# Attention probabilities scaled ahead of their transposes, instead of the attention output after its accumulation

## The chip, the cores and the metric

The kernel runs on one core of a Trainium2 chip. The metric is the device time of one execution in microseconds (us), as a median of several runs. A core has five engines with a queue each: TensorE (PE, matmuls and transposes), VectorE (DVE), ScalarE (ACT), GpSimd (POOL) and SyncE (SP, which issues most DMAs). Each engine takes its instructions in the order of the program; engines wait for one another on semaphores. TensorE reads SBUF and writes PSUM, which has eight banks of 128 x 512 fp32 here, all of them named in this kernel.

## The reference

Two layers over 512 tokens of width 1024. Each layer normalizes x, projects it (`w_in`), runs a recurrent group (RG-LRU) on half of the width and sparse attention (NSA) on the other half, gates both with silu, multiplies by `w_out` and adds x. A final norm follows. The attention part, cut to what the change touches:

```
o_cmp = softmax(q kc^T) vc          # 31 compressed positions
o_slc = softmax(q_rot ks^T) vs      # selected blocks: all of them at this length
o_win = softmax(q_rot kw^T) vw      # window of 512: plain causal at this length
gates = sigmoid(gate_logits)        # 3 per head and token
y_nsa = gates[0]*o_cmp + gates[1]*o_slc + gates[2]*o_win
y     = y_nsa * silu(g_nsa)         # then y @ w_out
```

There are 8 query heads of 64 in 2 key groups of 4. The gate and one over the row sum of the exponentials are one number per token, head and branch.

## The kernel before, in words

Everything follows one list of steps, `schedule()`. Each engine walks through the whole list and runs its own share of each step, so a step's place in the list is its place in every engine's queue. Projections are split in high and low fp32r parts, three matmuls for a product (L1351 to L1353), with weight chunks loaded by SP, split by ACT (`HI`, L774) and DVE (`LO`, L983).

`attention(l)` (L69) lists the attention of a layer. There are 16 units (tile `i` of 128 queries, branch `b` 0 or 1, pair of heads); a unit has four heads and `W = 128*(i+1)` keys. Unit by unit:

- `S` (two steps, r = 0 and 1): PE makes scores of two heads in the two `s_ps` banks (L1410, L1413), DVE takes their minimum (L1259), ACT the exponential into `probs` with its row sum (L928, which shows as an ACTIVATE and a read of the accumulator). `S` of unit u+1 is woven into the steps of unit u, at 0.2 and 0.6 of its length.
- `T`: for each 128 keys PE transposes the four heads' `probs` into a `t_ps` bank (L1426). The first `T` of a unit waits for all four exponentials of it. ACT and DVE in turn copy the bank into one of three `probsT` buffers (L937, L1267).
- `W`: PE multiplies `probsT` by the values (L1462) into an output bank. `C` steps are the same for the compressed branch (L1431), whose probabilities `CS2` has scaled already.
- `K`: DVE makes gate over row sum for the 8 heads of a tile and branch (L1271, L1274) and spreads it over 64 columns a head (L1276). `T` with `B`: PE transposes that spread tile (L1436), ACT copies it to `upad` (L947).
- `O`: DVE multiplies the output bank of a branch with it and sums the branches in `E` (L1285 to L1291). So a query tile has three accumulation groups, alternating between `o_ps` and `a_ps`.
- `Y`, `YH`, `YL`: once the last `O` of a tile is done, DVE multiplies by silu (L1297), ACT and DVE split the result in high and low (L866, L1165).

Between these, `fill()` puts pieces of other matmuls of the layer (`F`, and `G` of the last layer, L1372 to L1374), so that PE has work while the attention's chain runs: per unit four, later three and two pieces in layer 0, five and later four in layer 1. Eight pieces follow the last unit. `put_later` places the steps that come some positions behind another one. After layer 0, PE's `ON` pieces need all `YL` of the layer; after layer 1, the last tile's `G` pieces do (L1364).

Of the kernel before, what the change touches and what calls it, by code (L numbers as in the profile page):

```python
# [28 lines left out]
P = 128  # L29
# [20 lines left out]
N_STAGE, N_RING, N_PT, N_E, N_SWP = 4, 3, 3, 6, 2  # L50
# [18 lines left out]
def attention(l):  # L69
# [27 lines left out]
    def put_later(steps):  # L97
# [9 lines left out]
        def finish(n, i):  # L107
            due.setdefault(n, []).append(("Y", l, i))
            due.setdefault(n + 2, []).append(("YH", l, "n", i))
            due.setdefault(n + 5, []).append(("YL", l, "n", i))  # L110

        n = 0
        while n < len(steps) or any(at >= n for at in due):
            if n < len(steps):
# [27 lines left out]
            if n >= len(steps) and waiting and not any(at >= n for at in due):  # L142
# [4 lines left out]
                   [("CS2", l)], *fill(per_unit[-1] - 2)])  # L147
    for u, (i, b, pair) in enumerate(units):
        main = []
        for k in range(i + 2):  # L150
            if k <= i:
                main.append([("T", l, ("P", i, b, pair, k))])
            if k == 0 and pair == 1:
                main[-1].append(("K", l, i, b))
# [113 lines left out]
class Plan:  # L268


    def __init__(self, sched):
# [5 lines left out]
        for st in sched:  # L277
# [24 lines left out]
            elif k == "O" and st[3] == 0:  # L302
# [34 lines left out]
        self.data = [key for key in self.turns if key[1] != "B"]  # L337
        self.data_no = {key: n for n, key in enumerate(self.data)}
        self.groups = [st[1:] for st in sched if st[0] == "O"]
        self.group_no = {key: n for n, key in enumerate(self.groups)}  # L340
        self.coefs = [st[1:] for st in sched if st[0] == "K"]
        self.coef_no = {key: n for n, key in enumerate(self.coefs)}

# [33 lines left out]
def hybrid_trunk(nc, x, norm_g, w_in, conv_w, conv_b, lru_wa, lru_ba, lru_wi, lru_bi, lru_lambda,  # L377
# [5 lines left out]
    rope_no, unit_no, turn_no, data_no, group_no = plan.rope_no, plan.unit_no, plan.turn_no, plan.data_no, plan.group_no  # L383

    ctx = ExitStack()
    with ctx:
# [15 lines left out]
        probsT = sb("probsT", [P, N_PT + 1, SEQ])  # L402
# [21 lines left out]
        mn, rs, coef = sb("mn", [P, 2, 4]), sb("rs", [P, 2, 8]), sb("coef", [P, 8])  # L424
# [14 lines left out]
        sq_tmp, sq_acc, spread_c = swp[:, 0, :], upad[:, CONV_W - 1:], upad[:, CONV_W - 1:]  # L439
# [4 lines left out]
        wide_c = probsT[:, N_PT, :]  # L444
# [36 lines left out]
        min_ok, exp_ok, coef_ok, spread_ok, o_done = sem("min_ok"), sem("exp_ok"), sem("coef_ok"), sem("spread_ok"), sem("o_done")  # L481
# [58 lines left out]
        def wait_turned(eng, key):  # L540

            d = data_no[key]
            eng.wait_ge(pt_dve if d % 2 else pt_act, d // 2 + 1)

        def wait_turn_bank(eng, n):

            if n >= 2:
                old = plan.turns[n - 2]
                if old[1] == "B":
                    eng.wait_ge(spread_ok, plan.coef_no[(old[0], old[2], old[3])] + 1)  # L550
                else:
                    wait_turned(eng, old)

        def o_bank(l, i, b):

            return o_banks[group_no[(l, i, b)] % 2]
# [143 lines left out]
        def _(pool):  # L700
# [51 lines left out]
            for st in sched:  # L752
# [4 lines left out]
                elif kind == "NORM":  # L757
                    root(st[1])
                elif kind == "FMEAN":
# [5 lines left out]
        def _(act):  # L765
# [45 lines left out]
            for st in sched:  # L811
# [85 lines left out]
                elif kind == "TURNE":  # L897
                    _, l, name = st
                    act.wait_ge(a_full, aux_no[("TURN", l, name)] + 1)
                    if l >= 1:  # L900
                        act.wait_ge(pv_done, per_layer(plan.data, l))
# [9 lines left out]
                elif kind == "S":  # L911
# [3 lines left out]
                    if r == 0:  # L915
# [6 lines left out]
                        if pair == 0 and (i >= 1 or l >= 1):  # L922
                            act.wait_ge(coef_ok, plan.coef_no[(l, i - 1, b) if i >= 1 else (l - 1, TT - 1, b)] + 1)
                    for g in range(N_KV):
                        n, j = 4 * u + 2 * r + g, 2 * g + r
                        act.wait_ge(min_ok, n + 1)
                        col = 2 * (2 * pair + r) + g
                        act.activation(probs[:, 4 * (u % 2) + j, 0:W], s_ps[g][:, 0:W], ACT.Exp, scale=-1.0,  # L928
                                       bias=mn[:, u % 2, j:j + 1], accum_out=rs[:, b, col:col + 1]).then_inc(exp_ok, 1)
                elif kind == "T":  # L930
                    key = (st[1], *st[2])
                    if key[1] != "B" and data_no[key] % 2 == 0:
                        n, d, rows = turn_no[key], data_no[key], P if key[1] == "P" else NC
                        act.wait_ge(t_full, n + 1)
                        if d >= N_PT:
                            act.wait_ge(pv_done, d - N_PT + 1)
                        act.activation(probsT[0:rows, d % N_PT, :], t_ps[n % 2][0:rows, :], ACT.Copy).then_inc(pt_act, 1)  # L937
                    elif key[1] == "B":
                        l, _, i, b = key
                        act.wait_ge(t_full, turn_no[key] + 1)  # L940
                        if b == 1:
                            act.wait_ge(o_done, group_no[(l, i, 0)] + 1)
                        elif i == 0:
                            act.wait_ge(conv_ok, CT * (l + 1))
                        else:
                            act.wait_ge(o_done, group_no[(l, i - 1, 1)] + 1)
                        act.activation(spread_c, t_ps[turn_no[key] % 2][:, :], ACT.Copy).then_inc(spread_ok, 1)  # L947
# [15 lines left out]
        def _(dve):  # L963
# [135 lines left out]
            for st in sched:  # L1099
# [160 lines left out]
                elif kind == "T":  # L1260
                    key = (st[1], *st[2])
                    if key[1] != "B" and data_no[key] % 2 == 1:
                        n, d, rows = turn_no[key], data_no[key], P if key[1] == "P" else NC
                        dve.wait_ge(t_full, n + 1)
                        if d >= N_PT:
                            dve.wait_ge(pv_done, d - N_PT + 1)
                        dve.tensor_copy(probsT[0:rows, d % N_PT, :], t_ps[n % 2][0:rows, :]).then_inc(pt_dve, 1)  # L1267
                elif kind == "K":
                    _, l, i, b = st
                    dve.wait_ge(exp_ok, 4 * (unit_no[(l, i, b, 1)] + 1))  # L1270
                    link(dve.reciprocal(coef[:, :], rs[:, b, :]))  # L1271
                    gate = gates[:, i, :].rearrange("p (g r b) -> p b r g", g=N_KV, b=3)[:, 1 + b, :, :]
                    c8 = coef[:, :].rearrange("p (r g) -> p r g", g=N_KV)
                    link(dve.tensor_tensor(c8, c8, gate, ALU.mult))  # L1274
                    c = coef[:, :].rearrange("p (h a) -> p h a", a=1).to_broadcast([P, 2 * GROUP, HD])
                    dve.tensor_copy(wide_c.rearrange("p (h a) -> p h a", a=HD), c).then_inc(coef_ok, 1)  # L1276
                elif kind == "O":
                    _, l, i, b = st
                    y = e_slot((l, f"y{i}"))
                    if b < 2:  # L1280
                        dve.wait_ge(spread_ok, plan.coef_no[(l, i, b)] + 1)
                    dve.wait_ge(pv_done, data_no[(l, "P", i, b, 1, i) if b < 2 else (l, "C", i, 1)] + 1)
                    if b == 0:
                        wait_e((l, f"y{i}"))
                        dve.tensor_tensor(y, o_bank(l, i, b)[:, :], spread_c, ALU.mult).then_inc(o_done, 1)  # L1285
                    elif b == 2:
                        dve.wait_ge(o_done, group_no[(l, i, 0)] + 1)
                        dve.tensor_tensor(y, y, o_bank(l, i, b)[:, :], ALU.add).then_inc(o_done, 1)
                    else:
                        link(dve.tensor_tensor(spread_c, o_bank(l, i, b)[:, :], spread_c, ALU.mult))  # L1290
                        dve.tensor_tensor(y, y, spread_c, ALU.add).then_inc(o_done, 1)  # L1291
                elif kind == "Y":
# [3 lines left out]
                    dve.wait_ge(o_done, group_no[(l, i, 1)] + 1)  # L1296
                    dve.scalar_tensor_tensor(out=e, in0=e, scalar=0.5, in1=silu_g[:, :, i * P:(i + 1) * P],  # L1297
                                             op0=ALU.mult, op1=ALU.mult).then_inc(ynsa_ok, 1)
# [29 lines left out]
        def _(pe):  # L1328
            def z_piece(key, p):
# [85 lines left out]
            def turn(key):  # L1415
# [4 lines left out]
                if key[1] == "P":  # L1420
                    _, _, i, b, pair, k = key
                    u = unit_no[(l, i, b, pair)]
                    if k == 0:
                        pe.wait_ge(exp_ok, 4 * (u + 1))
                    for j in range(4):
                        ins = pe.transpose(bank[:, j * P:(j + 1) * P], probs[:, 4 * (u % 2) + j, k * P:(k + 1) * P], ident[:, :])  # L1426
                elif key[1] == "C":
# [4 lines left out]
                else:  # L1432
                    _, _, i, b = key
                    pe.wait_ge(coef_ok, plan.coef_no[(l, i, b)] + 1)
# [182 lines left out]
```

## Time and profile before

| | us |
|---|---|
| median of 3 runs | 629.15 (627.08 to 630.05) |
| the profiled execution, its own time | 629.98 |
| its span, first to last instruction | 628.3 |
| PE busy | 584.3 |
| DVE busy | 402.6 |
| ACT busy | 294.1 |
| POOL busy | 16.0 |

Attention steps fill about 148 to 300 us (layer 0) and 447 to 612 us (layer 1) of the span. "Busy" counts overlapping matmuls once. An instruction's mean is its duration, not its distance from the next of its kind: pipelined ones overlap. "idle [x <-releaser]" is the time in which the engine had nothing to run before an instruction, and what ended it.

### The profile page before, as it was taken

To read this page: it belongs to the slowest core of one execution; us is meant where nothing else is said; L and a number is where in the kernel's file an instruction comes from. 1 tells how busy PE (TensorE), PEld (TensorE's weight loads), DVE (VectorE), ACT (ScalarE), POOL (GpSimd) and SP (SyncE) were. 2 spreads that over 40 slices of the span, in tenths; PEclk is the share of its full clock that TensorE was granted. 3 is DMA by queue.
4 is the path that set the end of the run, shared out by engine and by line. 5 is a ranking of instruction groups with operands and counts; after the bars stand their busy time and mean duration, and the time that the engine had idled before them with its cause. 6 is when DMAs were issued, how large, how long until landed. Compare 5 with 4: busy or idle time off the path is not lost.

```text
span 628.3 us, 8688 instructions
## 1 busy us (share of the span) xinstructions
PE 584.3 (93%) x3207; PEld 409.1 (65%) x3207; DVE 402.6 (64%) x690; ACT 294.1 (47%) x586; POOL 16.0 (3%) x32
## 2 busy tenths in 40 slices
PE   4999999889999989998999999999899999999994
PEld 3776777667556555555788677777776666555563
DVE  4786966776555664755576679667664766557532
ACT  3647654424444452543453574462344545445522
POOL 1000000000000000000230000000000000000000
PEclk9999999998999998999899999998999999999999
DMA  8755393343111110101232745734421112000112
GB/s 243 201 155 152 87 231 85 84 102 104 56 34 34 34 35 1 34 0 35 67 101 70 198 122 145 142 82 99 110 74 35 34 39 64 0 2 1 34 34 68
DMA packets 94889, 50.71 MB, mean 81 GB/s; under 512 B 42992, under 2 KB 92288, under 8 KB 94848
## 3 DMA queue, kind: packets, MB, share of 16 engines
q1 hardware_dynamic: 91456, 45.95, 28.9%
q10 hardware_dynamic: 3392, 4.21, 2.5%
q8 instruction: 26, 0.43, 0.3%
q14 instruction: 15, 0.12, 0.1%
HBM read 44.90 MB, written 2.10 MB: 75 GB/s over the span
## 4 chain that ended last, share of the span: by engine, by line
PE 65%; DVE 13%; ACT 8%; DMA 5%; issue 5%; ACTq 2%; POOLq 0%; POOL 0%; DVEq 0%
PE z_ps L1351 10%; PE z_ps L1353 9%; PE z_ps L1352 9%; PE s_ps L1410 6%; PE t_ps L1426 5%; PE a_ps L1462 5%; DMA swp<-E 4%; PE o_ps L1462 3%; ACTq L837 2%; PE o_ps L1351 2%; PE o_ps L1352 2%; PE o_ps L1353 2%; ACT probs L928 2%; PE s_ps L1413 2%; DVE w_lo L983 2%
## 5 line engine op out<-in xcount | busy, mean ns | idle before, releaser
L1351 PE MATMUL z_ps<-h_hi,w_hi 128*128 128x512 f32 x264 | 111.1, 421 | 3.1 <-DVE h_lo L976 2.2
L928 ACT ACTIVATE probs<-s_ps,mn 128x128 f32<-128x128 f32 (+3 forms) x128 | 66.3, 523 | 99.7 <-DVE mn L1259 87.5
L1353 PE MATMUL z_ps<-h_hi,w_lo 128*128 128x512 f32 x264 | 103.6, 393 | 0.0
L1352 PE MATMUL z_ps<-h_lo,w_hi 128*128 128x512 f32 x264 | 103.6, 392 | 0.0
L774 ACT ACTIVATE w_hi<-stage 128x1024 fp32r<-128x1024 f32 x58 | 61.0, 1054 | 74.2 <-PE z_ps L1353 44.8
L1259 DVE TENSOR_REDUCE mn<-s_ps 128x1 f32<-128x128 f32 (+3 forms) x128 | 56.8, 485 | 52.0 <-PE s_ps L1413 51.9
L983 DVE TENSOR_TENSOR w_lo<-stage,w_hi 128x1024 fp32r<-128x1024 f32 x58 | 71.1, 1226 | 11.1 <-ACT w_hi L774 10.0
L1351 PEld LDWEIGHTS z_ps<-h_hi,w_hi 128*128 128x128 f32 x264 | 49.9, 189 | 22.4 <-issue 14.5
L1353 PEld LDWEIGHTS z_ps<-h_hi,w_lo 128*128 128x128 f32 x264 | 49.8, 189 | 11.1
L1267 DVE COPY probsT<-t_ps 128x512 f32<-128x512 f32 (+1 forms) x48 | 32.9, 686 | 36.1 <-PE t_ps L1426 24.8
L1352 PEld LDWEIGHTS z_ps<-h_lo,w_hi 128*128 128x128 f32 x264 | 50.1, 190 | 7.9 <-issue 0.2
L1410 PE MATMUL s_ps<-k_st,q_st 64*128 64x128 f32 (+3 forms) x384 | 47.2, 351 | 3.5 <-ACT probs L928 3.4
L1426 PE MATMUL t_ps<-ident,probs 128*128 128x128 f32 x320 | 49.3, 280 | 0.3 <-ACT probs L928 0.2
L1426 PEld LDWEIGHTS t_ps<-ident,probs 128*128 128x128 f32 x320 | 36.0, 141 | 15.3 <-issue 11.9
L1410 PEld LDWEIGHTS s_ps<-k_st,q_st 64*128 64x128 f32 x384 | 28.9, 187 | 24.5 <-issue 14.5
L937 ACT ACTIVATE probsT<-t_ps 128x512 f32<-128x512 f32 (+1 forms) x48 | 28.4, 592 | 34.9 <-PE t_ps L1426 34.8
L1351 PE MATMUL o_ps<-h_hi,w_hi 128*128 128x512 f32 x104 | 43.4, 417 | 0.0
L1353 PE MATMUL o_ps<-h_hi,w_lo 128*128 128x512 f32 x104 | 41.9, 403 | 0.0
L1352 PE MATMUL o_ps<-h_lo,w_hi 128*128 128x512 f32 x104 | 41.8, 402 | 0.0
L1462 PE MATMUL a_ps<-probsT,v_sb 128*64 128x256 f32 x192 | 30.9, 403 | 0.5 <-DVE probsT L1267 0.5
L1351 PE MATMUL z_ps<-y_hi,w_hi 128*128 128x512 f32 x64 | 31.0, 484 | 0.0
L1032 DVE TENSOR_TENSOR E<-z_ps,rstd 128x512 f32<-128x512 f32 x23 | 15.8, 689 | 19.3 <-PE z_ps L1353 17.3
(220 smaller groups left out, 904.0 us busy)
## 6 DMA issues: line engine op xcount, KB each, us to landing
stage<-in_w_in SPq DMA_DIRECT2D x28, 512.0 KB, 4.2
stage<-in_w_in SPq DMA_DIRECT2D x32, 256.0 KB, 4.0
stage<-in_cmp_k_w SPq DMA_DIRECT2D x8, 512.0 KB, 3.9
stage<-in_cmp_v_w SPq DMA_DIRECT2D x8, 512.0 KB, 5.0
stage<-in_w_out SPq DMA_DIRECT2D x8, 512.0 KB, 3.4
stage<-in_w_out SPq DMA_DIRECT2D x16, 256.0 KB, 3.9
swp<-E ACTq DMA_DIRECT2D x48, 64.0 KB, 2.1
out<-xT SPq DMA_DIRECT2D x8, 256.0 KB, 2.5
```

The source lines that it names most:

```text
L774: act.activation(split_into(n)[0], stage_of(key), ACT.Copy).then_inc(hi_split, 1)
L928: act.activation(probs[:, 4 * (u % 2) + j, 0:W], s_ps[g][:, 0:W], ACT.Exp, scale=-1.0, bias=mn[:, u % 2, j:j + 1], accum_out=rs[:, b, col: ...
L937: act.activation(probsT[0:rows, d % N_PT, :], t_ps[n % 2][0:rows, :], ACT.Copy).then_inc(pt_act, 1)
L983: dve.tensor_tensor(lo, stage_of(plan.split[n]), hi.bitcast(F32), ALU.subtract).then_inc(lo_dve, 1)
L1259: dve.tensor_reduce(mn[:, u % 2, j:j + 1], s_ps[g][:, 0:W], AX.X, ALU.min).then_inc(min_ok, 1)
L1267: dve.tensor_copy(probsT[0:rows, d % N_PT, :], t_ps[n % 2][0:rows, :]).then_inc(pt_dve, 1)
L1351: pe.matmul(bank, w_hi[:, slot, at:at + P], x_hi, start=first, stop=False)
L1352: pe.matmul(bank, w_hi[:, slot, at:at + P], x_lo, start=False, stop=False)
L1353: ins = pe.matmul(bank, w_lo[:, slot, at:at + P], x_hi, start=False, stop=last)
L1410: pe.matmul(s_ps[g][:, 0:W], q_st[rows, GROUP * of_q + at, i * P:(i + 1) * P], k_st[rows, b, of_k, 0:W], start=(part == 0), stop=False)
L1426: ins = pe.transpose(bank[:, j * P:(j + 1) * P], probs[:, 4 * (u % 2) + j, k * P:(k + 1) * P], ident[:, :])
L1462: ins = pe.matmul(o_bank(l, i, b)[g * HD:(g + 1) * HD, pair * N_PAIR_COL:(pair + 1) * N_PAIR_COL], v, probsT[0:rows, d % N_PT, g * 2 * P:( ...
```

## The change

Each unit's probabilities are multiplied by gate over row sum before they are transposed, in a new step `N`. VectorE computes the four coefficients of the unit and scales heads 0 and 1, GpSimd scales heads 2 and 3, in place in `probs`. The first `T` of the unit now waits for both. `N` of unit u+1 lies at 0.9 of unit u's steps, behind `S` and ahead of the unit's first `T`. The steps `K`, `T B` and `O` are gone with their banks' handover; the three branches of a query tile accumulate in one bank, which alternates by tile, and `Y` reads that bank. `Y` comes three steps after the tile's last `W` at the earliest, `YH` one and `YL` three steps behind it. In the diff the first `N` branch is GpSimd's and the second VectorE's. `probsT` has four buffers for the data, where it had three and one for the spread coefficients.

```diff
         def finish(n, i):
             due.setdefault(n, []).append(("Y", l, i))
-            due.setdefault(n + 2, []).append(("YH", l, "n", i))
-            due.setdefault(n + 5, []).append(("YL", l, "n", i))
+            due.setdefault(n + 1, []).append(("YH", l, "n", i))
+            due.setdefault(n + 3, []).append(("YL", l, "n", i))
...
-                if st[0] == "W" and st[2][0] == "P" and st[2][3:] == (1, st[2][1]):
-                    _, i, b, _, _ = st[2]
-                    due.setdefault(n + 1 + b, []).append(("T", l, ("B", i, b)))
-                    due.setdefault(n + 4 + 2 * b, []).append(("O", l, i, b))
-                    if b == 1:
-                        waiting.append((n + 9, i))
-                if st[0] == "W" and st[2][0] == "C" and st[2][2] == 1:
-                    due.setdefault(n + 3, []).append(("O", l, st[2][1], 2))
+                if st[0] == "W" and st[2][0] == "P" and st[2][2:] == (1, 1, st[2][1]):
+                    waiting.append((n + 2, st[2][1]))
...
-        s += flat_list(weave(main, (ahead, 0.0, 0.8), (fill(per_unit[u]), 0.0, 1.0)))
+        norm = [[("N", l, units[u + 1])]] if u + 1 < len(units) else []
+        s += flat_list(weave(main, (ahead, 0.0, 0.8), (fill(per_unit[u]), 0.0, 1.0), (norm, 0.8, 1.0)))
...
+                elif kind == "N":
+                    _, l, unit = st
+                    u, W = unit_no[(l, *unit)], P * (unit[0] + 1)
+                    pool.wait_ge(coef_ok, u + 1)
+                    for j in (2, 3):
+                        rows = probs[:, 4 * (u % 2) + j, 0:W]
+                        ins = pool.tensor_scalar(rows, rows, coef[:, u % 2, j:j + 1], None, ALU.mult)
+                    ins.then_inc(norm_pool, 1)
...
+                elif kind == "N":
+                    dve.wait_ge(exp_ok, 4 * (u + 1))
+                    link(dve.reciprocal(coef[:, u % 2, :], rs[:, u % 2, :]))
...
+                    dve.tensor_tensor(c4, c4, gate, ALU.mult).then_inc(coef_ok, 1)
+                    dve.wait_ge(coef_ok, u + 1)
+                    for j in (0, 1):
+                        rows = probs[:, 4 * (u % 2) + j, 0:W]
+                        ins = dve.tensor_scalar(rows, rows, coef[:, u % 2, j:j + 1], None, ALU.mult)
+                    ins.then_inc(norm_dve, 1)
...
                     if k == 0:
-                        pe.wait_ge(exp_ok, 4 * (u + 1))
+                        pe.wait_ge(norm_dve, u + 1)
+                        pe.wait_ge(norm_pool, u + 1)
...
+                first, last = (b, pair, k) == (0, 0, 0), (b, pair, k) == (1, 1, i)
+                if first and TT * l + i >= 2:
+                    pe.wait_ge(ynsa_ok, TT * l + i - 1)
```

## Rows read from the trace of the kernel before

**Rows 1.** Stretches: span, then busy of PE, PEld, DVE, ACT, POOL, granted clock, DMA share.
```profile
148.00:300.00 152.00, 141.68 (x883) 87.68 (x883) 90.99 (x169) 69.49 (x182) 0.00 (x0) 0.97 0.12 32
447.00:612.00 165.00, 163.06 (x1008) 105.38 (x1008) 99.06 (x183) 76.65 (x197) 1.10 (x2) 1.00 0.12 35
```
**Rows 2.** Waits of PE over the span: total us, times, longest.
```profile
PE z_ps L1366 <- DVE q_st L1165: 3.6, 1, 3.6
PE s_ps L1410 <- ACT probs L928: 3.4, 6, 0.9
...
PE t_ps L1431 <- ACT upad L947: 3.2, 4, 1.9
PE z_ps L1351 <- DVE q_st L1165: 3.1, 1, 3.1
...
PE t_ps L1436 <- ACT probsT L937: 0.3, 1, 0.3
PE t_ps L1426 <- ACT probs L928: 0.2, 1, 0.2
```
**Rows 3.** Groups by line: busy us, mean ns, idle before.
```profile
L1436 PE MATMUL t_ps<-ident,probsT 128*128 128x128 f32 x64 | 9.7, 273 | 0.3 <-ACT probsT L937 0.3
L1276 DVE COPY probsT<-coef 128x512 f32<-128x512 f32 x16 | 6.8, 427 | 0.5
L1291 DVE TENSOR_TENSOR E<-E,upad 128x512 f32<-128x512 f32 x8 | 5.5, 694 | 0.3
L1325 DVE TENSOR_SCALAR xT<-xT,fin_rt 128x512 f32<-128x512 f32 x4 | 1.9, 481 | 0.7 <-POOL fin_rt L762 0.7
L993 DVE TENSOR_SCALAR probs<-ident,rt 128x128 f32<-128x128 f32 x8 | 1.7, 281 | 1.1 <-POOL rt L749 1.1
L741 POOL TENSOR_TENSOR upad<-upad,swp 128x512 f32<-128x512 f32 x7 | 8.4, 1194 | 12.0 <-ACT swp L784 12.0
L738 POOL COPY upad<-swp 128x512 f32<-128x512 f32 x1 | 0.7, 672 | 280.3 <-ACT swp L784 280.3
L710 POOL TENSOR_SCALAR_AFFINE_SELECT ident<-ident 128x128 f32<-128x128 f32 x1 | 0.3, 293 | 0.2 <-POOL ident L709 0.2
```
**Rows 4.** Timeline around a unit's first transposes: start, duration; W = 128, 512, 512.
```profile
161.49 0.20 ACT L928 ACTIVATION_READ_ACCUMULATOR probs<-s_ps,mn 128x1 f32 x1
...
162.64 0.60 PE L1426 MATMUL t_ps<-ident,probs 128*128 128x128 f32 x4
...
284.02 0.20 ACT L928 ACTIVATION_READ_ACCUMULATOR probs<-s_ps,mn 128x1 f32 x1
284.25 0.20 DVE L1271 RECIPROCAL coef<-rs 128x8 f32<-128x8 f32 x1 [0.32 <-ACT probs L928]
...
284.57 1.09 PE L1426 MATMUL t_ps<-ident,probs 128*128 128x128 f32 x8
284.69 0.43 DVE L1276 COPY probsT<-coef 128x512 f32<-128x512 f32 x1
...
595.23 0.20 ACT L928 ACTIVATION_READ_ACCUMULATOR probs<-s_ps,mn 128x1 f32 x1
...
596.45 0.66 PE L1426 MATMUL t_ps<-ident,probs 128*128 128x128 f32 x4
```
**Rows 5.** Timeline after layer 0's attention: a VectorE and a GpSimd instruction together.
```profile
314.54 1.67 DVE L976 SCALAR_TENSOR_TENSOR h_lo<-xT,par,h_hi 128x512 fp32r<-128x512 f32 x1
...
314.57 1.09 POOL L741 TENSOR_TENSOR upad<-upad,swp 128x512 f32<-128x512 f32 x1 [1.63 <-ACT swp L784]
...
317.61 0.75 DVE L976 SCALAR_TENSOR_TENSOR h_lo<-xT,par,h_hi 128x512 fp32r<-128x512 f32 x1 [0.79 <-ACT h_hi L781]
```
**Rows 6.** Stretches with PE idle, columns as in Rows 1.
```profile
234.00:242.00 8.00, 7.95 (x34) 4.91 (x34) 1.53 (x3) 1.05 (x2) 0.00 (x0) 0.57 0.21 52
298.00:304.00 6.00, 4.32 (x13) 3.51 (x14) 1.63 (x2) 0.55 (x1) 0.00 (x0) 0.72 0.32 87
611.00:616.00 5.00, 1.42 (x9) 0.99 (x8) 2.99 (x6) 2.04 (x4) 0.54 (x1) 1.00 0.29 86
```

More of the change, by code:

```diff
@@ L146, in attention @@
     s = flat_list([[("S", l, units[0], 1)], *fill(2), [("TURN", l, LAST), ("TURNE", l, LAST)],
-                   [("CS2", l)], *fill(per_unit[-1] - 2)])
+                   [("N", l, units[0])], [("CS2", l)], *fill(per_unit[-1] - 2)])
     for u, (i, b, pair) in enumerate(units):
@@ L301, in __init__ @@
                 self.e.append(st[1:])
-            elif k == "O" and st[3] == 0:
+            elif k == "Y":
                 self.e.append((st[1], f"y{st[2]}"))
@@ L401, in hybrid_trunk @@
         probs = sb("probs", [P, 8, SEQ])
-        probsT = sb("probsT", [P, N_PT + 1, SEQ])
+        probsT = sb("probsT", [P, N_PT, SEQ])
         q_st = sb("q_st", [P, 8, SEQ], F32R)
@@ L540, in wait_turned, with o_bank @@
         def wait_turned(eng, key):
[L542 to L543 removed]
+            n = turn_no[key]
+            eng.wait_ge(pt_dve if n % 2 else pt_act, n // 2 + 1)
         def wait_turn_bank(eng, n):
             if n >= 2:
[L548 to L556, printed above, removed]
+                wait_turned(eng, plan.turns[n - 2])
+        def o_bank(l, i):
+            return o_banks[(TT * l + i) % 2]
         def flat_in(eng, l, kv, g):
@@ L926, in _ @@
                         act.wait_ge(min_ok, n + 1)
-                        col = 2 * (2 * pair + r) + g
                         act.activation(probs[:, 4 * (u % 2) + j, 0:W], s_ps[g][:, 0:W], ACT.Exp, scale=-1.0,
-                                       bias=mn[:, u % 2, j:j + 1], accum_out=rs[:, b, col:col + 1]).then_inc(exp_ok, 1)
+                                       bias=mn[:, u % 2, j:j + 1], accum_out=rs[:, u % 2, j:j + 1]).then_inc(exp_ok, 1)
                 elif kind == "T":
                     key = (st[1], *st[2])
-                    if key[1] != "B" and data_no[key] % 2 == 0:
-                        n, d, rows = turn_no[key], data_no[key], P if key[1] == "P" else NC
+                    n, rows = turn_no[key], P if key[1] == "P" else NC
+                    if n % 2 == 0:
                         act.wait_ge(t_full, n + 1)
[L935 to L947, printed above, removed]
+                        if n >= N_PT:
+                            act.wait_ge(pv_done, n - N_PT + 1)
+                        act.activation(probsT[0:rows, n % N_PT, :], t_ps[n % 2][0:rows, :], ACT.Copy).then_inc(pt_act, 1)
                 elif kind == "ON":
@@ L1261, in _ @@
                     key = (st[1], *st[2])
-                    if key[1] != "B" and data_no[key] % 2 == 1:
-                        n, d, rows = turn_no[key], data_no[key], P if key[1] == "P" else NC
+                    n, rows = turn_no[key], P if key[1] == "P" else NC
+                    if n % 2 == 1:
                         dve.wait_ge(t_full, n + 1)
[L1265 to L1291, printed above, removed]
@@ new lines, in _ @@
+                        if n >= N_PT:
+                            dve.wait_ge(pv_done, n - N_PT + 1)
+                        dve.tensor_copy(probsT[0:rows, n % N_PT, :], t_ps[n % 2][0:rows, :]).then_inc(pt_dve, 1)
+                elif kind == "N":
+                    _, l, unit = st
+                    i, b, pair = unit
+                    u, W = unit_no[(l, *unit)], P * (i + 1)
+                    dve.wait_ge(exp_ok, 4 * (u + 1))
+                    link(dve.reciprocal(coef[:, u % 2, :], rs[:, u % 2, :]))
+                    gate = gates[:, i, :].rearrange("p (g r b) -> p b g r", g=N_KV, b=3)[:, 1 + b, :, 2 * pair:2 * pair + 2]
+                    c4 = coef[:, u % 2, :].rearrange("p (g r) -> p g r", g=N_KV)
+                    dve.tensor_tensor(c4, c4, gate, ALU.mult).then_inc(coef_ok, 1)
[4 more added lines that the diff above has]
+                    ins.then_inc(norm_dve, 1)
@@ L1431, in turn @@
                         ins = pe.transpose(bank[0:NC, j * P:(j + 1) * P], sc[:, i, 2 * (2 * pair + j % 2) + j // 2, :], ident[:, :])
-                else:
-                    _, _, i, b = key
-                    pe.wait_ge(coef_ok, plan.coef_no[(l, i, b)] + 1)
-                    for r in range(GROUP):
-                        ins = pe.transpose(bank[:, r * P:(r + 1) * P], wide_c[:, r * P:(r + 1) * P], ident[:, :])
                 ins.then_inc(t_full, 1)
             def weigh(key):
-                l, d = key[0], data_no[key]
+                l, n = key[0], turn_no[key]
                 wait_turned(pe, key)
@@ L1444, in weigh @@
                     _, _, i, b, pair, k = key
-                    last = pair == 1 and k == i
                 else:
                     _, _, i, pair = key
-                    b, k, last = 2, 0, pair == 1
-                first = pair == 0 and k == 0
-                group = group_no[(l, i, b)]
-                if first and group >= 2:
-                    pe.wait_ge(o_done, group - 1)
-                if first and group - per_layer(plan.groups, l) < 2:
+                    b, k = 2, 0
+                first, last = (b, pair, k) == (0, 0, 0), (b, pair, k) == (1, 1, i)
+                if first and TT * l + i >= 2:
+                    pe.wait_ge(ynsa_ok, TT * l + i - 1)
+                if first and i < 2:
                     pe.wait_ge(z_dve, plan.freed(plan.z, z_no[("Z", l, LAST)])[1])
@@ L1460, in weigh @@
                         v, rows = vc_sb[:, g, :], NC
-                    ins = pe.matmul(o_bank(l, i, b)[g * HD:(g + 1) * HD, pair * N_PAIR_COL:(pair + 1) * N_PAIR_COL], v,
-                                    probsT[0:rows, d % N_PT, g * 2 * P:(g + 1) * 2 * P],
+                    ins = pe.matmul(o_bank(l, i)[g * HD:(g + 1) * HD, pair * N_PAIR_COL:(pair + 1) * N_PAIR_COL], v,
+                                    probsT[0:rows, n % N_PT, g * 2 * P:(g + 1) * 2 * P],
                                     start=first, stop=last, skip_group_check=True)
```

37 lines of the change are left out of this document (14 added, 23 removed).

## The prediction

> **What bounds the kernel now.** I first read the page's busy times and then the stretches. TensorE is busy in 141.7 of 152 us of layer 0's attention and in 163.1 of 165 us of layer 1's; VectorE has about 60% in both, GpSimd nothing [rows 1]. So TensorE's queue sets the end. What is taken from it is a gain, and each new wait in it is a loss, since it takes its work in order. The waits of PE come next: those that the change touches are short, and none is a standing wait for the exponentials [rows 2]. Last I read, unit by unit in the timeline, the distance between a unit's last exponential and its first transposes, because the new step lies exactly there.
>
> **What goes.** (1) The transposes of the spread coefficients: 64 of 0.27 us each [rows 3], which overlap; four start within 0.44 us on the chain of waits, so 16 x 0.44 = 7.0 us of PE. (2) Waits that exist only for them: 3.2 us for the copy to `upad` and 0.3 us before L1436 [rows 2], 3.5 us. (3) At the end of each layer PE waits for the last tile's low half: 3.1 us before `ON`, 3.6 us before the last `G` [rows 2]. The chain T B, copy, O, O, Y, YH, YL becomes Y, YH, YL, about 2.1 us (0.69 + 0.63 + 0.69, the durations of L1297, L866 and L1165), and starts some three steps behind the last `W`, beside eight pieces of 0.69 us, 5.5 us. Both waits go: 6.7 us. What is late next is nothing on PE: the last `G`'s bank was free 5 us before its use. (4) TensorE's clock: behind two of these gaps the granted clock falls to its lower level, 0.57 over 8 us and 0.72 over 6 us [rows 6]. 43% of 8 us is 3.4 us; of the second, 1.5 us fall on time in which PE works. 4.9 us. Together 7.0 + 3.5 + 6.7 + 4.9 = 22.1 us.
>
> **What VectorE and ScalarE get.** ACT loses 16 copies of 0.59 us, off the path. DVE loses L1271 and L1274 (16 x 0.37 us), L1276 (6.8 us [rows 3]) and 32 products and sums of 0.69 us such as L1291 [rows 3], in all 34 us (16 `O` steps of branches 0 and 2, 8 of branch 1 with two each). It gains 32 x 0.37 us and 64 scalings. A scaling of 512 columns in SBUF takes 0.48 us (L1325), one of 128 columns 0.28 us (L993) [rows 3]; with 0.35 and 0.41 between, the mean is 0.38 and the sum 24.3 + 11.8 = 36 us. DVE's total hardly changes, and at 60% it isn't the bound. I put that at nothing; if it should queue ahead of the minima, it is in the range.
>
> **What the new step costs.** Before, the first `T` of a unit needs the four exponentials. Now it needs them and then, one after another: reciprocal, product with the gate, two scalings. PE has nothing else in its queue that it may run. DVE's queue holds behind the waiting reciprocal the copies of later transposes, evictions and splits; these are needed later than the first `T`, so PE feels it first.
> - From the end of the exponentials to the coefficient: reciprocal at 284.25, the next but one at 284.69 [rows 4], 0.44 us, and about 0.06 us ahead of it: 0.5 us.
> - Two scalings on GpSimd. The trace has none. The nearest rows: a copy of 128 x 512 takes 0.67 us, a sum with two inputs 1.19 us, an operation with 128 columns 0.29 us [rows 3]. It has one tensor input like the copy but a scalar to fetch, so for 512 columns I take 0.9 us, between them, for 128 columns 0.3, and a line between: 0.5 at 256, 0.7 at 384. DVE's two scalings (0.28 to 0.48 each) are shorter and go beside it.
> - The two engines don't run freely together: DVE's L976 takes 0.75 us alone, and 1.67 us beside a GpSimd sum of 1.09 us that started with it [rows 5]. I add 0.3 us for one engine waiting for a scaling of the other.
> This makes 1.4, 1.8, 2.2 and 2.6 us for W = 128, 256, 384, 512. From below: copy price and 0.1 us for a handover, 1.2, 1.4, 1.7, 1.9 us. From above: all four scalings one after another, 0.5 + 2 x (GpSimd + DVE): 1.7, 2.2, 2.7, 3.3 us. A gain is excluded, since nothing starts earlier for it.
>
> Against that stands the slack that PE's own queue gives. I read it in the timeline for all 30 units behind the first of a layer, as start of the first transposes minus end of the last accumulator read: 0.95 us for the first (W = 128), 0.35 us for the last of layer 0, 1.02 us for the last of layer 1 [rows 4]. Where a `T B` or its wait stood in between I took it off. Layer 0 in us: 0.95, 1.9, 2.4 | 0.15, 1.2, 1.8, 1.4 | 1.0, 0.25, 0.9, 0.25 | 0.14, 0.35, 1.4, 0.35 by width; layer 1: 0.9, 2.1, 2.4 | 1.5, 0.74, 2.5, 2.0 | 1.0, 0.66, 2.2, 0.95 | 0.6, 1.0, 2.3, 1.0. The slack is small where few fill pieces lie behind `S` at 0.6 of the unit, and the step is longest there. Stall = cost minus slack where positive: W 128: 0.95 us in both layers, 256: 4.0, 384: 10.4, 512: 13.7. Sum 29.0 us (17.7 and 11.3). From below 18.2 us, from above 41.6 us.
>
> The clock again: gaps of 1.9 and 3.1 us were followed by a fall, one of 3.6 us at 611 us was not [rows 6]. About 12 of the new stalls are over 1.5 us, each with PE busy before and behind it. I take two falls of 1.7 us, 3.4 us (0 to 12).
>
> The Trainium skill has a rule that bears on the last point of the cost: "SBUF — State Buffer", section "Who interferes with whom", says that GpSimd and VectorE share one port pair as an exclusive lock for a whole instruction, and that `tensor_scalar` in SBUF can enter a mode that takes it. Rows 5 agree with a lock (1.67 is about 0.75 + 1.09 less an overlap). By that rule the change's split over two engines buys little: all scalings stand in a row. That is the second rival below. For the price alone, "GPSIMD Engine Reference", section 3.1, gives 769 ns for 512 elements in its best loop; by it the cost at 512 would be 2.3 instead of 2.6 us.
>
> **Sum.** 629.98 (the profiled execution) - 22.1 + 29.0 + 3.4 = 640.3 us. That execution was 0.8 us over the median, so against the median: 639.5 us.
>
> **Rivals.**
> - Faster, by the queue ahead of the exponentials. With `K` and `O` gone from DVE, minima and so exponentials may come earlier. PE waits 3.4 us for exponentials at L1410 [rows 2], so that queue is tight. With 0.5 us more slack at each unit and the lower cost, I get 9.4 us of stalls and no fall of the clock: 629.98 - 22.1 + 9.4 - 0.8 = 616.5 us. It decides once the cost less the gained slack is under about 1.9 us at 512 columns. Against it: the minima before most of these units started within 0.1 us of their scores' end, so there is little to win. 0.2.
> - The lock in full. All scalings in a row: 41.6 us of stalls, 629.98 - 22.1 + 41.6 + 3.4 - 0.8 = 652 us. For it: rows 5; against it: DVE's scalings may slip in while GpSimd starts up. 0.2.
> - It cancels out: lower cost, slack as read, two falls: 629.98 - 22.1 + 18.2 + 3.4 - 0.8 = 628.7 us. For it: the copy is the row most like the scaling. 0.15.
> - My forecast, 639.5 us with its own range of 633 to 647: 0.45.
>
> **Chances and range.** A measurement tells about 0.5%, 3.1 us, from no change: faster is under 626.0, slower over 632.3. Faster 0.20, within 0.15, slower 0.45 + 0.20 = 0.65. The range goes from 622 (half of the first rival left out) to 655 (a tenth above, where the clock falls oftener): it takes in both bounds of the cost.
>
> **What would show it.** Right: a wait of PE at L1426's successor for POOL's or DVE's scaled `probs` as its largest, near 29 us over some 22 units, largest for the wide tiles and larger in layer 0; no wait for `q_st` at both layers' ends; PE some 7 us less in transposes; POOL's scaling of 512 columns between 0.67 and 1.2 us. Wrong: that wait under 15 us, or minima that come earlier against their scores; a GpSimd scaling outside these bounds; longer attention of DVE behind the reciprocal, seen as PE waiting for `probsT` copies; more than three falls of the clock.

## The result and the profile after

| us | before | after |
|---|---|---|
| median beside each other | 629.6 (627.08 to 635.31) | 727.68 (725.62 to 728.99) |
| span of the profiled execution | 628.3 | 725.7 |
| mean granted clock of TensorE | 0.985 | 0.931 |
| PE busy | 584.3 | 610.4 |
| DVE busy | 402.6 | 413.0 |
| POOL busy | 16.0 | 91.5 |

The ratio is 1.157, with a 95% interval of 1.153 to 1.161. The change makes the kernel 98 us slower. The forecast had the direction, but 639.5 us, and its range ended at 655.

The waits of PE in the kernel after (total us, times, longest), its largest and those that answer to [rows 2]:

```profile
PE t_ps L1395 <- POOL probs L747: 77.1, 28, 4.8
PE a_ps L1538 <- DVE E L1006: 4.1, 3, 1.7
...
PE s_ps L1378 <- ACT probs L915: 3.5, 5, 2.1
...
PE o_ps L1424 <- ACT probsT L924: 1.4, 2, 0.7
```

One wait is new, in front of nearly every unit's first transposes, and it is 77 of the 98 us. The waits for `q_st` and `upad` of [rows 2] are gone. The scalings by form (busy us, mean ns, idle before), GpSimd's and then VectorE's:

```profile
L747 POOL TENSOR_SCALAR probs<-probs,coef 128x512 f32<-128x512 f32 x16 | 27.2, 1707 | 96.6 <-DVE coef L1253 96.6
L747 POOL TENSOR_SCALAR probs<-probs,coef 128x384 f32<-128x384 f32 x16 | 21.5, 1353 | 75.5 <-DVE coef L1253 75.5
L747 POOL TENSOR_SCALAR probs<-probs,coef 128x256 f32<-128x256 f32 x16 | 16.6, 1045 | 69.2 <-DVE coef L1253 69.2
L747 POOL TENSOR_SCALAR probs<-probs,coef 128x128 f32<-128x128 f32 x16 | 10.2, 647 | 308.9 <-DVE coef L1253 308.9
```
```profile
L1257 DVE TENSOR_SCALAR probs<-probs,coef 128x512 f32<-128x512 f32 x16 | 10.5, 701 | 0.3
...
L1257 DVE TENSOR_SCALAR probs<-probs,coef 128x128 f32<-128x128 f32 x16 | 4.8, 340 | 0.3
```

GpSimd takes 1.71 us for 512 columns, where I had put 0.9. Two typical units in the timeline (start, duration) show how the wait is made. In the first, VectorE is free:

```profile
302.80 0.20 ACT L915 ACTIVATION_READ_ACCUMULATOR probs<-s_ps,mn 128x1 f32 x1
303.03 0.18 DVE L1250 RECIPROCAL coef<-rs 128x4 f32<-128x4 f32 x1 [0.32 <-ACT probs L915]
303.24 0.17 DVE L1253 TENSOR_TENSOR coef<-coef,gates 128x4 f32<-128x4 f32 x1
303.44 1.31 DVE L1257 TENSOR_SCALAR probs<-probs,coef 128x512 f32<-128x512 f32 x2
303.50 3.39 POOL L747 TENSOR_SCALAR probs<-probs,coef 128x512 f32<-128x512 f32 x2 [10.80 <-DVE coef L1253]
...
307.04 1.07 PE L1395 MATMUL t_ps<-ident,probs 128*128 128x128 f32 x8 [3.62 <-POOL probs L747]
```

From the last exponential (303.00) to the first transposes 4.04 us pass: 0.50 to GpSimd's start, 3.39 for its two scalings, 0.15 for the handover. VectorE is done at 304.75, 2.3 us before the transposes. In the second (W = 256) VectorE comes late:

```profile
200.86 0.20 ACT L915 ACTIVATION_READ_ACCUMULATOR probs<-s_ps,mn 128x1 f32 x1
...
202.59 0.69 DVE L1009 TENSOR_TENSOR E<-z_ps,rstd 128x512 f32<-128x512 f32 x1 [2.25 <-PE z_ps L1321]
...
203.32 0.18 DVE L1250 RECIPROCAL coef<-rs 128x4 f32<-128x4 f32 x1
...
203.79 1.98 POOL L747 TENSOR_SCALAR probs<-probs,coef 128x256 f32<-128x256 f32 x2 [9.82 <-DVE coef L1253]
...
205.92 0.87 PE L1395 MATMUL t_ps<-ident,probs 128*128 128x128 f32 x3 [3.36 <-POOL probs L747]
```

The exponentials end at 201.06, and VectorE stands idle. Its next instruction is the eviction L1009, which waits until 202.56 for a fill matmul of PE; the reciprocal stands behind it and starts at 203.32 instead of 201.1.

The clock, in stretches (span, busy of PE, PEld, DVE, ACT, POOL, granted clock, DMA share) through one stall and what follows:

```profile
303.00:307.00 4.00, 0.42 (x4) 0.00 (x0) 1.66 (x4) 0.00 (x0) 3.39 (x2) 1.00 0.00 0
307.00:311.00 4.00, 3.96 (x21) 2.11 (x21) 1.68 (x3) 0.77 (x2) 0.00 (x0) 0.62 0.00 0
311.00:315.00 4.00, 4.00 (x17) 2.54 (x15) 0.31 (x1) 1.87 (x5) 0.00 (x0) 0.53 0.00 0
315.00:319.00 4.00, 4.00 (x30) 2.30 (x28) 2.14 (x4) 1.32 (x4) 0.00 (x0) 1.00 0.02 4
319.00:323.00 4.00, 1.42 (x11) 0.38 (x8) 2.68 (x6) 0.59 (x3) 2.50 (x2) 0.83 0.00 0
323.00:327.00 4.00, 2.96 (x14) 2.40 (x14) 0.69 (x1) 0.60 (x1) 0.89 (x1) 0.50 0.00 0
```
```profile
322.00:323.00 1.00, 0.00 (x0) 0.00 (x0) 0.00 (x0) 0.00 (x0) 1.00 (x2) 0.50 0.00 0
```

PE idles from 303.4 to 307.0. In this stall the clock stays full and falls behind it: in the next 8 us PE is busy throughout, at 0.62 and 0.53, and 17 matmuls stand in 4 us where at the full clock there are 30 (not all of one kind). In the next unit's stall, 320.8 to 324.0, the clock falls while PE is still idle (the last row) and is low when PE starts again. The trace has 22 stretches at the lower clock: twelve begin within 1.5 us behind a gap of PE of over 1 us, nine inside such a gap, and one behind PE's last work.

### The profile page after: what moved, and what is told of

It is laid out like the page before. It is cut to its first block, busy times and chain, and to the rows that moved or that the text cites. A ratio compares the mean times of both kernels' runs of the same rounds, so it can differ in the third digit from the quotient of the medians.

```text
span 725.7 us, 8574 instructions
## 1 busy us (share of the span) xinstructions
PE 610.4 (84%) x3143; PEld 423.0 (58%) x3143; DVE 413.0 (57%) x738; ACT 286.3 (39%) x570; POOL 91.5 (13%) x96
## 4 chain that ended last, share of the span: by engine, by line
PE 53%; DVE 15%; POOL 10%; ACT 9%; DMA 6%; issue 5%; ACTq 2%; POOLq 0%; DVEq 0%; SPq 0%
POOL probs L747 10%; PE z_ps L1319 8%; PE z_ps L1320 7%; PE z_ps L1321 7%; PE t_ps L1395 7%; PE s_ps L1378 6%; DMA swp<-E 4%; ACT probs L915 3%; PE a_ps L1424 3%; ACTq L827 2%; DVE w_lo L960 2%; PE o_ps L1319 2%; PE o_ps L1321 2%; PE o_ps L1320 2%; PE s_ps L1381 2%
## 5 line engine op out<-in xcount | busy, mean ns | idle before, releaser
L747 POOL TENSOR_SCALAR probs<-probs,coef 128x128 f32<-128x128 f32 (+3 forms) x64 | 75.5, 1188 | 550.2 <-DVE coef L1253 550.2
L1395 PE MATMUL t_ps<-ident,probs 128*128 128x128 f32 x320 | 60.8, 326 | 77.2 <-POOL probs L747 77.1
L1319 PE MATMUL z_ps<-h_hi,w_hi 128*128 128x512 f32 x264 | 113.9, 432 | 3.5 <-DVE h_lo L953 2.7
L1321 PE MATMUL z_ps<-h_hi,w_lo 128*128 128x512 f32 x264 | 106.1, 402 | 0.0
L1320 PE MATMUL z_ps<-h_lo,w_hi 128*128 128x512 f32 x264 | 106.1, 402 | 0.0
L1395 PEld LDWEIGHTS t_ps<-ident,probs 128*128 128x128 f32 x320 | 44.2, 168 | 98.0 <-issue 92.8
L1378 PE MATMUL s_ps<-k_st,q_st 64*128 64x128 f32 (+3 forms) x384 | 54.4, 394 | 3.7 <-ACT probs L915 3.5
L1378 PEld LDWEIGHTS s_ps<-k_st,q_st 64*128 64x128 f32 x384 | 33.3, 214 | 28.1 <-issue 18.9
L1319 PE MATMUL z_ps<-y_hi,w_hi 128*128 128x512 f32 x64 | 33.8, 528 | 0.0
L1424 PE MATMUL a_ps<-probsT,v_sb 128*64 128x256 f32 x192 | 32.5, 422 | 0.4 <-DVE probsT L1244 0.4
```

What stands on the lines that cost most here:

```text
L747: ins = pool.tensor_scalar(rows, rows, coef[:, u % 2, j:j + 1], None, ALU.mult)
L1319: pe.matmul(bank, w_hi[:, slot, at:at + P], x_hi, start=first, stop=False)
L1320: pe.matmul(bank, w_hi[:, slot, at:at + P], x_lo, start=False, stop=False)
L1321: ins = pe.matmul(bank, w_lo[:, slot, at:at + P], x_hi, start=False, stop=last)
L1378: pe.matmul(s_ps[g][:, 0:W], q_st[rows, GROUP * of_q + at, i * P:(i + 1) * P], k_st[rows, b, of_k, 0:W], start=(part == 0), stop=False)
L1424: ins = pe.matmul(o_bank(l, i)[g * HD:(g + 1) * HD, pair * N_PAIR_COL:(pair + 1) * N_PAIR_COL], v, probsT[0:rows, n % N_PT, g * 2 * P:(g + ...
```

## The experiments

The theory: the loss is the wait for the scalings (GpSimd's price, plus the late reciprocal) and the clock that falls behind it. The rivals: VectorE and GpSimd lock one another out of SBUF; the new order of evictions and banks costs it. Each kernel is the one after the change with the edit shown. Each was timed beside the kernel before on the same chip (medians of it 627.6 to 630.3 us), and its ratio is to that.

**Without the scalings.** The four multiplications are left out of the computation.

```diff
-    for j in (2, 3): ... pool.tensor_scalar(...)      # and DVE's j in (0, 1)
-    pe.wait_ge(norm_dve, u + 1); pe.wait_ge(norm_pool, u + 1)
+    pe.wait_ge(coef_ok, u + 1)
```

> The changed kernel without the four scalings of a unit (they are left out of the computation; reciprocal, product with the gate, and the first transposes' wait for the coefficient stay). Theory A (the loss is the scalings' price, plus evictions that stand ahead of the reciprocal in VectorE's queue, plus the clock that falls behind the stalls): stalls at the first transposes shrink from 77 to about 12 us, the removed work is worth its 17 us, the clock stays up: 618 to 626 us. Theory B (one accumulation bank for a tile, or the new order of steps, costs by itself): 650 us or more, with PE waiting somewhere else than at the first transposes.

Measured: 630.0 us, ratio 1.002 (0.998 to 1.006). That is above the 618 to 626 us expected, and far under the 650 of the rival theory. The scalings and what hangs on them are the whole 98 us. But it is no gain either: the coefficient alone is still late for PE:

```profile
PE t_ps L1385 <- DVE coef L1249: 11.7, 12, 1.8
...
PE s_ps L1369 <- ACT probs L911: 4.9, 7, 1.8
```

By my table of slack a cost of 0.65 us without scalings would stall PE for 2.5 us; it is 11.7, so about 9 us come from the late reciprocal alone. In the trace 10.4 us of such waits stand before units whose reciprocal starts over 0.6 us late, and 1.5 before all others. These 11.7 us and 1.5 us more before the scores take back 13.2 of the 17.4 us of work and waits that the change removes, so the shared bank and the new order of steps can cost a few us at most; that they cost nothing is not shown.

**All four scalings on VectorE.**

```diff
-    for j in (0, 1):      # DVE; GpSimd's two are gone
+    for j in (0, 1, 2, 3):
```

> All four scalings of a unit on VectorE, GpSimd idle. Theory A: a scaling of 512 columns costs 0.4 to 0.6 us there from start to start, so coefficient to transposes takes 2.1 to 2.9 us at W = 512 where it took 3.9; with the queue ahead of the reciprocal unchanged the stalls are 43 to 56 us by the sum over the 30 units, and the time 660 to 685 us. Theory C (what costs is that a step stands in the chain at all, not GpSimd's price): within 10 us of 727.

Measured: 675.9 us, 1.077 (1.070 to 1.084), clock 0.962, a time inside the band of the theory. Four in a row on one engine beat two beside two, since each is 0.48 us:

```profile
L1253 DVE TENSOR_SCALAR probs<-probs,coef 128x512 f32<-128x512 f32 x32 | 13.4, 482 | 0.3
...
L1253 DVE TENSOR_SCALAR probs<-probs,coef 128x128 f32<-128x128 f32 x32 | 7.0, 282 | 0.3
```
```profile
PE t_ps L1390 <- DVE probs L1253: 42.4, 26, 3.2
```

**GpSimd's two alone.** VectorE's two are left out of the computation.

```diff
-    for j in (0, 1): ... dve.tensor_scalar(...)
-    pe.wait_ge(norm_dve, u + 1)
```

> VectorE's two scalings of a unit are left out of the computation; GpSimd's two stay, and the first transposes wait for them alone. Theory A (the price is GpSimd's own): its scaling of 512 columns stays at 1.7 us, the stalls near 77 us, the time 718 to 728 us. Rival L (the port lock of the prediction: the two engines hold each other up): GpSimd's scaling falls to 0.7 to 1.2 us and the time to 690 us or less.

Measured: 721.0 us, 1.149 (1.142 to 1.156).

```profile
L747 POOL TENSOR_SCALAR probs<-probs,coef 128x512 f32<-128x512 f32 x16 | 24.8, 1562 | 96.8 <-DVE coef L1253 96.8
```
```profile
PE t_ps L1389 <- POOL probs L747: 70.7, 28, 4.5
```

The price is GpSimd's own. VectorE beside it adds 0.15 us to each in the mean at 512 columns (0.29 us to a unit's first, 1.85 instead of 1.56, and nothing to its second) and 6 to 7 us to the kernel.

**The clock.** PE fills its wait with transposes of the identity that nobody reads, as many per unit as its gap held.

```diff
+    pe.wait_ge(exp_ok, 4 * (u + 1))
+    for _ in range(count[u]):
+        pe.transpose(bank[:, 0:P], ident[:, :], ident[:, :])
     pe.wait_ge(norm_dve, u + 1)
```

> The changed kernel with added transposes of the identity into the bank that the unit's first transposes overwrite, placed in PE's wait for the scalings and as many as filled the stall of that unit (0 to 42 of 0.113 us, 704 in all). The stalls stay as long, but PE isn't idle in them. Theory A with the clock as a third term of about 38 us: the granted clock goes from 0.93 to over 0.98 and the time to 690 to 700 us. Rival: the fallen clock lay mostly on time in which PE waited anyway, so it costs little: 715 to 730 us.

Measured: 693.1 us, 1.104 (1.097 to 1.111), mean clock 0.992. The unit shown above, now at 290 us:

```profile
290.46 3.71 PE L1394 MATMUL t_ps<-ident 128*128 128x128 f32 x32
...
290.62 3.40 POOL L747 TENSOR_SCALAR probs<-probs,coef 128x512 f32<-128x512 f32 x2 [9.15 <-DVE coef L1253]
294.16 1.06 PE L1398 MATMUL t_ps<-ident,probs 128*128 128x128 f32 x8
```
```profile
294.00:298.00 4.00, 4.00 (x29) 2.61 (x27) 1.98 (x3) 1.39 (x4) 0.01 (x1) 1.00 0.02 4
```

The first transposes come no earlier behind the last exponential (4.05 us here; over all 32 units the distances differ by 0.3 us in sum), yet 34.6 us are back. That is what the low clock cost against a kernel that has almost none of it; the kernel before had some of its own (0.985), so the change's part is a few us less.

**The reciprocal earlier.**

```diff
-    (norm, 0.8, 1.0)
+    (norm, 0.62, 0.62)
```

> The scaling step directly behind the unit's second score step (at 0.62 of the unit before, not 0.9), so ahead of the eviction of a fill matmul in VectorE's queue. Theory A: the reciprocal starts within 0.05 us of the last exponential in nearly all units (11 of 31 start over 0.6 us late now, 24 us in all), stalls 53 to 60 us instead of 77, time 690 to 708 us. Rival: VectorE now blocks on the exponentials with transposes' copies behind it, PE waits for those instead, and the time stays within 10 us of 727.

Measured: 700.1 us, 1.115 (1.108 to 1.121), clock 0.938.

```profile
PE t_ps L1395 <- POOL probs L747: 39.8, 23, 4.1
PE a_ps L1424 <- DVE probsT L1244: 14.0, 8, 3.0
```

As expected. The reciprocal now starts 0.03 us behind the last exponential in every unit. 77.1 us of stalls become 53.8; a part moved to the `probsT` copies, which now stand behind `N` on VectorE. The place in VectorE's queue is worth 23 us of waits and 28 us of time.

**GpSimd with another instruction.**

```diff
-    pool.tensor_scalar(rows, rows, coef[:, u % 2, j:j + 1], None, ALU.mult)
+    pool.tensor_tensor(rows, rows, coef[:, u % 2, j:j + 1].to_broadcast([P, W]), ALU.mult)
```

> GpSimd multiplies by the coefficient broadcast as a second tensor input, not as a per-partition scalar operand. Its sum with two inputs took 1.09 to 1.19 us for 512 columns. If the slow part is the form with a scalar operand, a scaling falls from 1.7 to about 1.15 us, the stalls from 77 to about 50 us by the sum over the units, and the time to 675 to 695 us. If every product there is as slow, 1.7 us or more and 727 us or more. VectorE's scalings keep their time in either case.

Measured: 699.9 us, 1.116 (1.108 to 1.125). GpSimd gained what was expected, and VectorE lost, which was not; the time missed the expected band of 675 to 695 us:

```profile
L747 POOL TENSOR_TENSOR probs<-probs,coef 128x512 f32<-128x512 f32 x16 | 17.7, 1129 | 98.9 <-DVE coef L1253 98.9
```
```profile
L1257 DVE TENSOR_SCALAR probs<-probs,coef 128x512 f32<-128x512 f32 x16 | 20.3, 1311 | 0.3
```
```profile
299.38 2.54 DVE L1257 TENSOR_SCALAR probs<-probs,coef 128x512 f32<-128x512 f32 x2
299.42 2.22 POOL L747 TENSOR_TENSOR probs<-probs,coef 128x512 f32<-128x512 f32 x2 [11.50 <-DVE coef L1253]
```
```profile
PE t_ps L1395 <- DVE probs L1257: 54.7, 27, 3.8
```

A scaling of VectorE takes 0.48 us alone, 0.70 in the mean beside GpSimd's `tensor_scalar`, 1.31 beside its two-input product. Here PE waits for VectorE.

**All on VectorE, with room.** The next unit's scores 0.2 of a unit earlier, `N` at 0.7.

```diff
-    for j in (0, 1):      # DVE; GpSimd's two are gone
+    for j in (0, 1, 2, 3):
-    (ahead, 0.0, 0.8) ... (norm, 0.8, 1.0)
+    (ahead, -0.18, 0.62) ... (norm, 0.7, 0.7)
```

> All four scalings on VectorE, and the score steps of the next unit moved ahead from 0.2 and 0.6 to 0.02 and 0.42 of a unit, the scaling step to 0.7. That gives PE 0.18 of a unit more work (1.2 to 1.8 us) between the scores and the first transposes, and puts the step ahead of the evictions near the unit's end. Theory A: stalls of 42 us in the version with all on VectorE fall to 5 to 15 us, the clock stays up, 618 to 635 us. Rival: two score steps so near one another make PE wait for the first's exponentials (2.2 us at 512 columns), and VectorE's queue blocks on the exponentials with copies behind it: 640 us or more.

Measured: 631.2 us, 1.006 (1.003 to 1.009). The wait for the scaled rows is 2.8 us; what is left waits for ScalarE's copies:

```profile
PE a_ps L1419 <- ACT probsT L920: 9.7, 12, 2.0
...
PE o_ps L1419 <- ACT probsT L920: 4.1, 5, 2.4
...
PE t_ps L1390 <- DVE probs L1253: 2.8, 5, 0.8
```

**One head on ScalarE.** As the last, with head 3 scaled by ScalarE (`activation` Copy with the coefficient as its scale).

```diff
+    act.wait_ge(coef_ok, u + 1)
+    rows = probs[:, 4 * (u % 2) + 3, 0:W]
+    act.activation(rows, rows, ACT.Copy, scale=coef[:, u % 2, 3:4]).then_inc(norm_pool, 1)
```

> As the version with score steps and scaling moved ahead, with heads 0 to 2 scaled on VectorE and head 3 on ScalarE. The step is about 0.4 us shorter at 512 columns. Theory A: 0 to 5 us under the version with all on VectorE. Rival: ScalarE's queue (weight splits waiting for PE) stands ahead of its scaling, or the exponentials behind it come later: 0 to 10 us over it.

Measured: 625.7 us, 0.997 (0.994 to 1.000), 5.5 us under the last version and no clear gain over the kernel before. The copies are still waited for, 14.3 us in all:

```profile
L929 ACT ACTIVATE probs<-probs,coef 128x512 f32<-128x512 f32 x8 | 5.8, 723 | 4.3 <-DVE coef L1255 4.1
```
```profile
PE a_ps L1426 <- ACT probsT L920: 10.2, 12, 2.0
PE s_ps L1380 <- ACT probs L911: 4.3, 4, 2.4
PE o_ps L1426 <- ACT probsT L920: 4.1, 5, 2.5
```

**Scores behind the first transposes.** Both kernels as the last, with the two scores of the next unit and `N` elsewhere.

```diff
-    (ahead, -0.18, 0.62) ... (norm, 0.7, 0.7)
+    (ahead, -0.03, 0.61) ... (norm, 0.72, 0.72)    # the first kernel
+    (ahead, -0.07, 0.73) ... (norm, 0.75, 0.75)    # the second
```

> As e9_dve_act, but the scores of the next unit at 0.13 and 0.45 of a unit (e9: 0.02 and 0.42) and the scaling at 0.72. Theory: the 14 us for which TensorE waits in e9_dve_act for ScalarE's copies to probsT come from the unit's first copy lying behind the exponentials of the first scores in ScalarE's queue; with the scores behind the first transposes the copy is ahead of them. Those waits fall to under 6 us, scaling waits rise to 1 to 4 us since the chain has less room: 616 to 623 us. Rival: the copies wait for ScalarE as a whole, wherever the scores stand; the waits stay near 14 us and the time within 0.5% of 625.7 us.

> As e10_s_behind_t, with the second scores at 0.53 and the scaling at 0.75. Theory: the copies gain as in e10_s_behind_t, but the chain of second scores, minima, exponentials and scalings has 0.08 of a unit less ahead of the first transposes (0.8 to 1 us), so 5 to 12 us of waits for the scaled rows come back: 620 to 632 us, slower than e10_s_behind_t. Rival: the chain has room enough either way and both take the same time.

Measured: 631.4 us, 1.005 (1.002 to 1.008), and 637.3 us, 1.014 (1.009 to 1.019). Both lie above their expected bands; that the second is the slower came true. In the first, then in the second:

```profile
PE s_ps L1380 <- ACT probs L911: 11.9, 18, 2.5
PE t_ps L1397 <- DVE probs L1259: 8.2, 12, 1.4
...
PE a_ps L1426 <- ACT probsT L920: 1.1, 3, 0.5
```
```profile
PE t_ps L1397 <- DVE probs L1259: 11.5, 15, 1.8
PE s_ps L1380 <- ACT probs L911: 7.0, 11, 2.5
```

The reason was right: the copies' 14.3 us fall to 1.8 (with 0.7 before `o_ps`). The time was not: against the last kernel 7.6 us came back as waits for exponentials and 7.4 as waits for scaled rows. In the second the waits for scaled rows are 3.3 us longer and those for exponentials 4.9 us shorter, so these two do not explain its 6 us more; that stays open.

**The copy first, in ScalarE's queue alone.** As with one head on ScalarE; PE and VectorE keep their order.

```diff
+    own = list(sched)        # ScalarE's walk only
+    # each first T of a unit is moved ahead of the next unit's first S, where it stood within 5 steps behind it
-    for st in sched:
+    for st in own:
```

> As e9_dve_act, TensorE's and VectorE's order unchanged; in ScalarE's queue alone the copy of a unit's first transposes stands ahead of the exponentials of the next unit's first scores. In e9_dve_act such a copy stood behind two exponentials although its bank was full 1.4 us before, and TensorE waited 14.3 us in 17 waits for these copies. Theory: more than half of the 14.3 us goes, and the exponentials come 0.6 us later where there is room: 614 to 622 us, faster than the kernel before by over 0.5%. Rival, as seen when the scores were moved: the 0.6 us comes back as waits for exponentials or scaled rows, and the time stays within 0.5% of 625.7 us.

Measured: 618.4 us, 0.983 (0.979 to 0.987): within the expected band, and faster than the kernel before and the one after the change.

```profile
PE s_ps L1387 <- ACT probs L918: 9.0, 11, 2.4
...
PE a_ps L1433 <- ACT probsT L927: 1.6, 5, 0.4
```

The waits for ScalarE's copies fall from 14.3 to 1.8 us (with 0.2 before `o_ps`), and those for exponentials rise by 4.7 us.

## Why the prediction was wrong

- **What bounds it** held: PE's queue sets the end, and of the 98 us 77.1 are one wait in it.
- **What goes** held in its kind. The 64 transposes and the waits of [rows 2] for `q_st` and `upad` (10.4 us with the two small ones) are gone. The 4.9 us of clock could not be had, since other stalls took it. In the version without scalings the 22.1 us are all but eaten by 11.7 us for the coefficient, 1.5 us more before the scores and a clock of 0.981, no better than before.
- **GpSimd's price** is the first step that failed. "for 512 columns I take 0.9 us, between them, for 128 columns 0.3" measured 1.71 and 0.65. My argument was that a scalar operand must lie between a copy (0.67) and a sum with two inputs (1.19 [rows 3]). It lies above both, 1.56 us even alone, so not even the bound from above (four scalings in a row, 3.3 us) held the 4.04 us. With the measured pairs of scalings (1.27, 1.98, 2.69, 3.39 us, plus 0.65) the costs are 1.92, 2.63, 3.34 and 4.04 us; less the slack that I read per unit the stalls are 2.0, 9.8, 19.5 and 25.2 us by width, 56 in all instead of 29.
- **VectorE's queue** is the second. I named what stands behind the waiting reciprocal and not what stands ahead of it. The reciprocal starts over 0.6 us late in 13 units, up to 3.43 us, 26 us in sum (I had read 11 units and 24 us before the early `N`). In eight of them it stands behind an eviction that waits for a matmul of PE, as in the unit at 201 us, in the other five behind splits and products that follow ScalarE's work. 56 + 26 = 82, above the 77.1 measured, as some of it falls into slack. The early `N` took 23 us of stalls back, about the same size. The slack table held: in the trace after the change (start of the first transposes, less PE's wait for them, less the end of the last read) 24 of its 30 values come out within 0.35 us, and the other six 0.4 to 1.3 us larger.
- **The clock** is the third. I wrote "I take two falls of 1.7 us, 3.4 us (0 to 12)". The mean granted clock fell from 0.985 over 628.3 us to 0.931 over 725.7 us. The missing share is 9.4 us before and 50.1 after; at the lower of the two levels, 1.2 instead of 2.4 GHz, that is 19 and 100 us of time, in 5 stretches before and 22 after. PE is busy in 16.6 us of them before and in 85.4 us after; at half the clock the 68.8 us more cost 34.4 us. Other readings come near. The 97.4 us of longer span - 77.1 + 10.4 (waits gone) + 7.0 (transposes gone) leave 37.7 us. PE's busy time is 610.4 - (584.3 - 7.0) = 33.1 us longer for the same work, which leaves 4.6 us of other idle time. Filling the gaps gave 34.6 us back. [rows 6] had gaps of 1.9 and 3.1 us with a fall behind each, and still I let only two of some 12 long stalls count. There were 28 stalls, of 2.8 us in the mean (77.1 / 28), 22 of them over 1.5 us.
- **The lock**: the Trainium skill ("SBUF — State Buffer", section "Who interferes with whom") has the two engines exclude one another. The scalings show part of it. In the unit at 303 us VectorE's two take 0.48 and 0.91 us where each takes 0.48 alone, and GpSimd's two 1.85 and 1.56 us where each takes 1.56 alone. But VectorE's second runs from 303.85 to 304.75, inside GpSimd's first (303.50 to 305.35), so neither is shut out for a whole instruction, and all four end in 3.45 us (303.44 to 306.89), where a lone pair of each, one behind the other, would need 0.88 + 3.10 = 3.98. So the rival of the lock in full fails for this instruction: with VectorE's share away the loss stays at 93 of 98 us. Beside the two-input product VectorE's pair takes 2.54 instead of 0.88 us. Whether the lock is full there stays open, since the product was never run without VectorE beside it. For the price the Trainium skill's "GPSIMD Engine Reference", section 3.1, gives 769 ns for 512 elements in its best loop; the trace has twice that, 1562 ns, without a neighbour.
- **The first rival** (a shorter queue ahead of the exponentials) didn't show: PE's wait for them is 3.5 us, 3.4 before.

Sum by its terms: 77.1 of stalls - 17.4 of work and waits removed + 37.7 of clock and rest = 97.4 us. The last term is a remainder; PE's busy time at the lower clock accounts for 34.4 of it, and the other 3 us are open. My sum had 29.0 - 22.1 + 3.4 = 10.3 us. Of the 87.1 us between, 48.1 are the stalls, 34.3 the clock and rest, and 4.7 the gain in clock that did not come. Why GpSimd's `tensor_scalar` is slower than its product isn't settled.

## What to carry to other kernels

Price a step put ahead of the bounding engine by its slowest engine in the instruction's own form, and where the trace has no row of that form, don't take a dearer-looking neighbour as the bound from above; here it was a scalar operand that cost more than a second tensor. Read what stands ahead of a new waiting instruction in its queue as closely as what stands behind it, and count the clock with repeated stalls of TensorE (here about 34 us on 77). When a chain has little slack, reordering one engine's own queue can gain where moving the step for all engines only shifts the wait, as it did here (618.4 us against 631.4 and 637.3).

## What the hardware showed that was not expected

- GpSimd's in-place `tensor_scalar` in fp32 with a scalar per partition takes 647 ns at 128 columns and 1707 at 512 beside VectorE; the line through these, 0.29 us + 2.76 ns a column, meets the widths between within 5% (1045, 1353 ns). Its product with the same scalar broadcast as a second input is a third shorter, 1129 ns at 512. VectorE takes 482 ns, ScalarE 723 ns (for its one head in the versions that use it).
- The same scaling on VectorE went from 482 to 701 or 1311 ns in the mean by what GpSimd ran beside it.
- TensorE's granted clock falls behind a stall of 3.6 us, to 0.62 and 0.53 over 8 us in which PE was busy throughout, or already inside one (0.50 at 322 us with PE idle). Only the low clock under PE's work costs time: 85.4 of about 100 us here.
